# An MLP in a decoder kernel: fused token groups, or seven block products over 512-token halves and a second phase from HBM

## What is computed

```python
D_MODEL = 1024; SEQ = 1024; D_FF = 4 * D_MODEL
def sq_relu_mlp(xn, w1, w2):
    return jnp.square(jax.nn.relu(xn @ w1)) @ w2
# each layer:  x += post_norm(sqrelu_mlp(pre_norm(x)))
```

## Time and profile before

| | |
|---|---|
| median of three runs | 3617.06 us (3616.76 to 3617.72) |
| span of the profiled execution | 3618.8 us |
| mean granted TensorE clock | 0.957 |
| PE busy | 3306.3 us, 91% of the span |
| DVE, ACT busy | 1765.0 us (49%), 1492.6 us (41%) |
| mean HBM rate | 94 GB/s |

### The profile page before, as it was taken

How to read it: one execution, slowest core, us unless ns; L and a number is a source line. 1 busy time by engine, 2 the same in 40 slices (tenths; PEclk the granted TensorE clock), 3 DMA queues, 4 the chain that set the end, 5 groups by cost and what they waited for, 6 DMA issues and landing times. The chain is left out here.

```text
span 3618.8 us, 44774 instructions
## 1 busy us (share of the span) xinstructions
PE 3306.3 (91%) x17479; PEld 2593.1 (72%) x17479; DVE 1765.0 (49%) x3075; ACT 1492.6 (41%) x2581; POOL 156.1 (4%) x168
## 2 busy tenths in 40 slices
PE   8869988876988999999999999998988999999996
PEld 6724643444786799899887677675786799899785
DVE  5576996623335444444444431066335444444443
ACT  6454553622344433433443431154334433433443
POOL 0021110033000000000000000012000000000000
PEclk9989998997989999999999999998999999999998
DMA  3123104056031433333352210012120433333353
GB/s 105 24 61 84 47 23 131 1 192 239 1 119 39 133 130 117 122 134 117 128 163 82 65 35 25 23 25 81 33 96 30 157 128 117 123 133 117 128 163 106
DMA packets 226199, 341.94 MB, mean 94 GB/s; under 512 B 34376, under 2 KB 163120, under 8 KB 225989
## 3 DMA queue, kind: packets, MB, share of 16 engines
q1 hardware_dynamic: 214212, 297.13, 25.4%
q0 software_dynamic: 11776, 41.95, 3.5%
HBM read 328.56 MB, written 10.19 MB: 94 GB/s over the span
## 5 line engine op out<-in xcount | busy, mean ns | idle before, releaser
L650 DVE TENSOR_TENSOR s_mlp_w2l<-s_mlp_w2b,s_mlp_w2h 128x1024 fp32r<-128x1024 f32 x192 | 235.2, 1226 | 582.3 <-ACT s_mlp_w2h L536 582.3
L179 PE MATMUL ps<-s_mlp_xl,s_mlp_w1h 128*128 128x384 f32 (+1 forms) x1536 | 497.3, 324 | 1.9 <-DVE s_mlp_xl L668 1.9
L181 PE MATMUL ps<-s_mlp_xh,s_mlp_w1h 128*128 128x384 f32 (+1 forms) x1536 | 494.3, 322 | 0.0
L180 PE MATMUL ps<-s_mlp_xh,s_mlp_w1l 128*128 128x384 f32 (+1 forms) x1536 | 493.6, 321 | 0.0
L536 ACT CAST s_mlp_w2h<-s_mlp_w2b 128x1024 fp32r<-128x1024 f32 x192 | 201.5, 1050 | 586.5 <-PE ps L181 586.4
L179 PE MATMUL ps<-s_mlp_w2l,s_mlp_hh 128*128 128x512 f32 x1024 | 404.5, 395 | 20.5 <-DVE s_mlp_hl L687 16.2
L181 PE MATMUL ps<-s_mlp_w2h,s_mlp_hh 128*128 128x512 f32 x1024 | 402.1, 393 | 0.0
L180 PE MATMUL ps<-s_mlp_w2h,s_mlp_hl 128*128 128x512 f32 x1024 | 402.1, 393 | 0.0
L179 PEld LDWEIGHTS ps<-s_mlp_xl,s_mlp_w1h 128*128 128x128 f32 x1536 | 288.3, 188 | 34.6 <-issue 28.4
L180 PEld LDWEIGHTS ps<-s_mlp_xh,s_mlp_w1l 128*128 128x128 f32 x1536 | 288.3, 188 | 6.2
L181 PEld LDWEIGHTS ps<-s_mlp_xh,s_mlp_w1h 128*128 128x128 f32 x1536 | 288.2, 188 | 0.0
(11 more groups left out here) (564 smaller groups left out, 5815.6 us busy)
## 6 DMA issues: line engine op xcount, KB each, us to landing
s_mlp_w1b<-w_ff SPq DMA_DIRECT2D x96, 1024.0 KB, 6.0
s_mlp_w2b<-w_ff SPq DMA_DIRECT2D x96, 1024.0 KB, 8.1
x_kb<-cache_mem_k SPq DMA_DIRECT2D x16, 512.0 KB, 6.7
x_vb<-cache_mem_v SPq DMA_DIRECT2D x2, 4096.0 KB, 21.3
s_orows_raw<-w_in_odd SPq DMA_DIRECT2D x32, 256.0 KB, 3.1
s_convsel_w<-w_in_even SPq DMA_DIRECT2D x12, 512.0 KB, 3.9
x<-x_prompt SPq DMA_DIRECT2D x8, 512.0 KB, 5.7
ev_mixT<-w_in_even SPq DMA_DIRECT2D x16, 256.0 KB, 4.2
```

The source lines that it names most:

```text
L179: nc.tensor.matmul(out, ah, bl, start=first, stop=False, skip_group_check=True)
L180: nc.tensor.matmul(out, al, bh, start=False, stop=False, skip_group_check=True)
L181: return nc.tensor.matmul(out, ah, bh, start=False, stop=last, skip_group_check=True)
L650: nc.vector.tensor_tensor(w2l[:, s % RING], w2b[:, c % 3, s % FC, :], w2h.bitcast(F32)[:, s % RING], ALU.subtract).then_inc(low2, 1)
```

## The change

The MLP is made in two phases, with all 1024 prompt tokens in each.

**First phase.** Two blocks of 128 hidden features (a pair, 256 columns of w1) are made at once. The contraction (1024) is cut in two, the pair in two, and the tokens in two halves of 512, and the eight block products are replaced by Strassen's seven (the form with shared sums). Each product is 4 blocks of the contraction by `times3`, 12 matmuls of 512 columns; 16 pairs x 7 = 112 products (N). The seven token operands (four of them sums, `sum_x`) are made and split once at the start, for all tokens (`XB`). Of the weights, each pair has three plain operands and four sums (`sum_w` on DVE); `round_w` (ACT) and `low_w` (DVE) split them six products ahead (LEAD) into a ring of eight slots. Products 3 and 7 of a pair go on summing in the bank of products 1 and 5, after ACT (`u1`) or DVE (`combine`) has read it. `combine` adds products to the four output blocks, `activate` rectifies and squares them in one instruction, and SP stores them to a scratch tensor in HBM (`hidden_scratch`), through a ring of six (`cr`). The sample tokens' features are made by plain float32 matmuls from the unrounded weights: `sample_up`, eight matmuls of 256 columns a pair in four column strips, then `fold`, two small matmuls that add the strips.

**Second phase.** The three groups stay (384, 384, now 256 tokens), 32 steps each, but only `down` and `down_sample` are left. In each step SP loads 128 rows of w2 (512 KB) and the hidden features of the group (192 KB, in the third group 128 KB) into rings of four. The tails of the first two groups are spread over three steps (`tail_at`), and eight banks are used in turn.

x itself is needed for the tails, but its place serves as work space. So `stage_out` stores each tile of x to HBM (`x_scratch`), the first phase scales x in place once that has landed (`G.spilled`), and the second phase loads the tiles back.

The core of it (SP, PE, and the order on ACT and DVE):

```diff
+            if spilled is not None:
+                for t in range(NT):
+                    sp.wait_ge(added, t + 2)
+                    sp.dma_start(G.xd[:, t, :], G.x[:, t, :]).then_inc(spilled, 16)
...
+            sp.dma_start(raw[:, 0], w1v[:, :, 0:2 * P]).then_inc(w1_in[0], 16)
+            sp.wait_ge(x_low, 21)
+            sp.dma_start(raw[:, 1], w1v[:, :, 2 * P:4 * P]).then_inc(w1_in[1], 16)
...
+            def load_w2(s):
+                f = s % NF
+                if s < 4:
+                    sp.wait_ge(product, N - 6)
+                else:
+                    sp.wait_ge(low2, s - 3)
+                if s - 4 >= 2 * NF:
+                    sp.wait_ge(sample_used, (s - 4 - 2 * NF) // 2 + 1)
+                sp.dma_start(w2b[:, s % 4], w2v[:, f, :]).then_inc(w2_in[s % 4], 16)
+
+            def load_h(s):
+                g, f = steps[s]
+                if s < 4:
+                    sp.wait_ge(product, N - 5)
+                else:
+                    sp.wait_ge(low_h, s - 3)
+                t0, n = groups[g]
+                sp.dma_start(hraw[:, s % 4, 0:n * P], G.hd[f, :, t0 * P:(t0 + n) * P]).then_inc(h_in[s % 4], 16)
...
+            for j in range(CR):
+                sp.wait_ge(stored[j], 16 * len(range(j, 4 * PAIRS, CR)))
+            sp.wait_ge(s_squared, PAIRS)
+            sp.dma_start(gB[:], bc(gain.rearrange("(o n) -> o n", o=1), [P, D])).then_inc(gain_row_in, 16)
+            for s in range(4, S_ALL):
+                load_w2(s)
+                load_h(s)
+                if s % 2 == 0 and s < 20:
+                    t = s // 2 - 2
+                    sp.dma_start(G.x[:, t, :], G.xd[:, t, :]).then_inc(x_in[t], 16)
...
+            for n in range(N):
+                p, i = divmod(n, 7)
+                if i == (3 if p == 0 else 0):
+                    sample_up(p)
+                if i == (5 if p == 0 else 2):
+                    fold(p)
+                multiply(n)
             for s in range(S_ALL):
-                if s + 1 < S_ALL:
-                    up(s + 1)
...
                 down(s)
                 if s >= 2 * NF and s % 2:
                     down_sample(s)
...
+            def round_w2(s):
...
+                    used_before(act, s - 2)
+                act.wait_ge(w2_in[s % 4], 16 * (s // 4 + 1))
+                nc.scalar.copy(w2h[:, s % 3], w2b[:, s % 4]).then_inc(high2, 1)
+            def round_h(s):
+                n = groups[steps[s][0]][1] * P
+                if s >= 2:
+                    used_before(act, s - 1)
+                act.wait_ge(h_in[s % 4], 16 * (s // 4 + 1))
+                nc.scalar.copy(hh[:, s % 2, 0:n], hraw[:, s % 4, 0:n]).then_inc(high_h, 1)
...
             for s in range(S_ALL):
                 if s + 2 < S_ALL:
                     round_w2(s + 2)
+                if s + 1 < S_ALL:
+                    round_h(s + 1)
+                if s in tail_at:
+                    tail(tail_at[s])
...
+            for k in range(4):
+                low_x(k, 0)
+                dve.wait_ge(gained, 4 * k + 4)
+                sum_x(k, 0, 1, 0)
+                sum_x(k, 1, 3, 1)
+                low_x(k, 1)
+                low_x(k, 2)
+                dve.wait_ge(x_summed, 4 * k + 1)
+                sum_x(k, 3, 3, 0)
+                dve.wait_ge(x_summed, 4 * k + 3)
+                sum_x(k, 2, 2, 3)
+                for j in range(3, 7):
+                    low_x(k, j)
+                if k == 1:
+                    low_w(0)
+                    low_w(1)
...
+            sum_w(1)
+            sum_w(2)
+            sum_w(4)
+            low_w(2)
...
             for s in range(S_ALL):
                 if s + 2 < S_ALL:
                     low_w2(s + 2)
+                if s + 1 < S_ALL:
+                    rest_of_h(s + 1)
```

More of the change, by code:

```diff
@@ L385, in stage_mlp @@
     NF = DFF // P
-    FC = 2
-    RING = 3
-    groups = [(3 * i, ROWS[3 * i:3 * i + 3]) for i in range(3)]
-    steps = [(g, j) for g in range(3) for j in range(NF)]
+    PAIRS = NF // 2
+    N = 7 * PAIRS
+    LEAD = 6
+    SLOTS = 8
+    CR = 6
+    B11, B21, T2, T1, T3, B22, T4 = range(7)
+    low_at = {B11: 0, B21: 1, B22: 2, T1: 3, T3: 4, T2: 5, T4: 6}
+    quarter_of = {B11: 0, T1: 0, T3: 1, B21: 2, T4: 2, B22: 3, T2: 3}
+    order_x = (B11, B21, B22, T1, T3, T2, T4)
+    groups = [(0, 3), (3, 3), (6, 2)]
@@ new lines, in stage_mlp @@
+        sums = space[:, 0:2048].rearrange("p (s n) -> p s n", s=4)
+        u1, u2, u4 = (space[:, 2048 + 512 * j:2560 + 512 * j] for j in range(3))
+        cr = space[:, 3584:3584 + 512 * CR].rearrange("p (s n) -> p s n", s=CR)
+        part = space[:, 6656:6912]
+        stmp = space[:, 6912:6976].rearrange("p (f t) -> p f t", f=2)
+        stack = space[:, 6976:6976 + NS]
+        full = [raw[:, 1].rearrange("p k n -> p (k n)").rearrange("p (q n) -> p q n", q=4),
+                H_.rearrange("p (q n) -> p q n", q=4)]
@@ new lines, in sample_up @@
+            def sample_up(p):
+                if p == 0:
+                    pe.wait_ge(xs_made, 1)
+                else:
+                    pe.wait_ge(s_rectified, p)
+                pe.wait_ge(w1_in[p % 2], 16 * (p // 2 + 1))
+                for k in range(KD):
+                    o = 32 * (k % 4)
+                    ins = nc.tensor.matmul(G.ps[o:o + NS, 7, 0:2 * P], xs[:, k, :], raw[:, p % 2, k, :], start=(k < 4), stop=(k >= 4),
+                                           tile_position=(0, o))
+                ins.then_inc(sampled, 1)
@@ new lines, in fold, with multiply @@
+            def fold(p):
+                pe.wait_ge(part_kept, p + 1)
+                if p == 0:
+                    pe.wait_ge(stack_in, 16)
+                for f in range(2):
+                    ins = nc.tensor.matmul(G.ps[:, 7, 256 + f * NS:256 + (f + 1) * NS], part[:, f * P:(f + 1) * P], stack,
+                                           start=True, stop=True)
+                ins.then_inc(folded, 1)
+            def multiply(n):
+                p, i = divmod(n, 7)
+                b = bank(p, (0, 1, 0, 2, 3, 4, 3)[i])
+                pe.wait_ge(w_low, n + 1)
+                if n == 3:
+                    pe.wait_ge(gained, 16)
+                a = 5 * p + (0, 1, 0, 2, 3, 4, 3)[i] - 7
+                if i not in (2, 6) and a >= 0:
+                    q, j = divmod(a, 5)
+                    if j == 0:
+                        pe.wait_ge(u2_kept, q + 1)
+                    else:
+                        pe.wait_ge(combined, 5 * q + (0, 1, 2, 5, 4)[j])
+                if i == 2:
+                    pe.wait_ge(u1_kept, p + 1)
+                if i == 6:
+                    pe.wait_ge(combined, 5 * p + 3)
+                for k in range(4):
+                    if n == 0 and k:
+                        warm(8)
+                    if p == 0:
+                        pe.wait_ge(x_low, 7 * k + low_at[i] + 1)
+                    ins = times3(nc, G.ps[:, b, :], slot(n, 0)[:, k], slot(n, 1)[:, k], XB[:, i, 0, k], XB[:, i, 1, k],
+                                 k == 0 and i not in (2, 6), k == 3)
+                ins.then_inc(product, 1)
@@ L710, in _ @@
             nc.vector.reciprocal(stat, rs[:]).then_inc(inverted, 1)
[L711 to L732 removed]
+            dve.wait_ge(inverted, 1)
```

562 lines of the change are left out of this document (327 added, 235 removed).

## The result

| | median | of runs | ratio to before |
|---|---|---|---|
| before | 3616.9 us | 3609.6 to 3617.7 | |
| changed kernel | 3723.2 us | 3715.2 to 3725.9 | 1.0292 [1.0277, 1.0307] |

The sign was as forecast, and the time lies in the range (3635 to 3728), at its upper end: 106 us are lost, where the forecast had 66. The profiled execution has a span of 3723.0 us.

A forecast was written before the change was run, and what follows sets the result against it. Both MLPs were taken to be bound by TensorE's matmuls, not HBM or the splitting engines. Terms summed to +32.8 us a layer, +65.6 for both, giving 3683 us, 1.8% slower; range 3635 to 3728.

The forecast's parts named there:

- The stand: Third group: PE waits 3.75 us per pair of steps for late w2 loads, 14 pairs, +52.5 us a layer.
- The bank hand-over: Rival, first phase: DVE late at product 7 or ACT at product 3, 16 or 32 us a layer, 3715 us; chance 0.06.
- the steady first phase: First phase: no added stall; DVE has 13 us of work in 20.6 us a pair.
- Start-up: First instruction to product 3: 42.6 us, plus 1.6 for lowered clock; +19 us a layer (15 to 24).
- The changes of group: Between phases and at group changes: waits of 6.3 us, before 10.2 and 1.6 for clock; -5.5 us a layer.
- The clock: Third group: lowered clock behind each stand costs 0.8 us, 14 times, +11 us a layer (0 to 22).
- I take half: Clock loss behind a 3.75 us stand set at 0.8 us, between stands of 2.30 and 5.78 us; the latter lost 1.6.
- the rival of 3728 us: Third group: PE restarts at the lower clock and stays there all step, 2.4 us a pair; 3728 us, chance 0.15.
- The price of a matmul: First phase: 1344 matmuls of 512 columns at 0.229 us, 307.8 us against 368.7, -60.9 us a layer.
- The sample's part: First phase: sample tokens by `sample_up`, `fold` and changes to float32, 1.4 us x 16, +22.4 us a layer (15 to 30).
- the model of the stage before: Sum of matmul prices and idle time for one MLP of the kernel before: 751 of the measured 758 us.
- the rival of hidden loads: Third group's loads are hidden, so +63.5 us a layer goes: 3556 us, faster by 1.7%; chance 0.10.

The follow-up runs named there:

- the kernel with both cures: Changed kernel with eight w2 buffers instead of four, and hidden features split ahead of rounding w2 in ACT's and DVE's queues: 3555.7 us, ratio 0.9831.

## Why the prediction was right, and where it was not

For layer 1, forecast and measured, in us. The second phase's first matmul starts at 3242.55, the third group's at 3507.86, its last sample product at 3695.40; the forecast for the third group is 384 x 0.229, 15 sample products, 52.5 and 11.

| term | forecast | measured |
|---|---|---|
| first instruction to product 3 | 42.6 | 44.75 |
| products 3 to 112 with the sample, and the clock behind product 3's start | 326.3 | 336.0 |
| groups one and two | 270 | 265.3 |
| third group | 166.4 | 187.5 |
| of that, stands, from start to start | 52.5 | 53.7 (51.4 idle) |
| of that, clock | 11 | 26 |

- **The stand: right in place, cause and size.** 3.75 us were forecast, 47.9 / 13 = 3.7 measured, fourteen times a layer, released by DVE's low part of the hidden features behind ACT's wait for the load. (The forecast counts from start to start, and so does the table; the profile counts the last matmul as busy to its end.) The two kernels that take the load's wait from ahead of the hidden features, by depth or by order, both lost the stand; the kernel before got it when its depth was cut.
- **The bank hand-over and the steady first phase: right.** In the second stretch PE is busy for all of 336.12 us.
- **Start-up: right within 2.2 us, its clock term by luck.** From the stage's first instruction to product 3 it is 44.75 us, where 42.6 was forecast:

```profile
2861.83 0.17 DVE L897 TENSOR_SCALAR stat<-stat 128x9 f32<-128x9 f32 x1 [1.66 <-PEq L74]
...
2906.58 0.47 PE L179 MATMUL ps<-s_mlp_XB,s_mlp_W 128*128 128x512 f32 x1 [2.02 <-DVE s_mlp_W L840]
...
2906.58:2916.00 9.42, 9.42 (x45) 6.76 (x46) 5.68 (x11) 3.06 (x6) 0.00 (x0) 0.82 0.25 60
```

  The 1.6 us for a lowered clock came too: the stretch behind product 3's start has a clock of 0.82, 1.7 us. But PE had stood for 2.02 us there (and for 4.00 ahead of product 1), not for the 6 that the forecast gave as the reason; behind 2.30 us in the earlier trace rows the clock had not fallen, so why it fell here is open.
- **The changes of group: right within 2.2 us.** The rest of that row is the price: 1152 matmuls took 0.2267 us each and not 0.229, 2.6 us less.
- **The clock: the mechanism right, the size wrong.** A pair takes 12.39 us where the one with TensorE kept busy takes 10.54, so a fall of the clock costs 1.85 us a stand instead of 0.8, 26 us instead of 11 a layer. The part that was mis-sized is "I take half", between a stand that had cost nothing and one of 5.78 us; the clock fell after every stand of 3.7. And the argument against the rival of 3728 us was false: slow matmuls would shorten the stand only if they lay between the load's issue and its use. They lie behind the stand and ahead of the next sample product, where they delay the issue itself. The rival had 2.4 us a pair, the trace 1.85: its case, a whole step at the lower clock, is what ten of the 28 stands show. The time ended 5 us from it, which is luck in part, since the first phase's matmuls and samples cost more than forecast and so made up for its dearer clock.
- **The price of a matmul: wrong for the first phase.** 0.229 was read from matmuls of the kernel before, whose operand pairs are all multiples of 512 bytes apart (w1h from xh: 90112). New buffers had a distance of 96 over, and the price was 0.2333: 1320 x 0.0043 = 6 us a layer. No row of before could have shown it: in its program all float32r matmuls but those of the query product have their operands at multiples of 512 bytes.
- **The sample's part: 1.6 us a pair, not 1.4** (1.2 for `sample_up`, 0.4 for `fold`, by what they add between the matmuls around them), 26 us a layer instead of 22.4, within the bounds given.
- The terms of the table are 28 us a layer above the forecast, and the result only 20: the model of the stage before fell 7 us short of its 758, and the forecast took the change from the model. Such misses that offset each other also make it luck in part that the kernel with both cures takes 3555.7 us, where the rival of hidden loads had 3556.
- The rule for a 512 KB load that the prediction takes from the Trainium skill (DMA: Bandwidth & Descriptors) is stated there for DMAs that GpSimd issues. SP issues these, and they took 3.64 and 3.72 us from issue to use; the forecast went by the first of these rows and not by the rule.

## What to carry to other kernels

In an in-order queue a wait for a load blocks all that stands behind it, so put what is due soonest ahead of what may wait (here worth 160 us); a deeper ring does the same for more memory. Price a stand of TensorE with the matmuls that run slowly behind it, and ask whether these delay the next issue. When matmuls of equal shape differ by 3%, look at the distance of their two operands' buffers.
